# A two-block transformer kernel on one core: roots of three norms applied behind the products, roots computed as columns, four query tiles, key scores one step behind, four expert units ahead

## What is computed

```python
def rms_norm(x, g): return x * rsqrt(mean(x * x, -1) + EPS) * g

# first_block, two layers
h = rms_norm(x, norm_g[l]) * (1.0 + scale) + shift        # scale, shift from cond @ ada_w
# layer 0: z = h @ even_w_in; convolution of 31 taps and RWKV-7 recurrence; @ even_w_out
# layer 1: z = h @ odd_w_in; q, k, v, index heads; top-256 keys of each query; 16 heads; @ odd_w_out
x = x + gate * out
x = rms_norm(x, final_g)

# second_block
proj = rms_norm(h, g_mix) @ w_in                          # b_gate, c_gate, v_conv, u_pool
y_conv = b_gate * conv3(c_gate * v_conv)
y_pool = (window_mean(u_pool) - u_pool) @ pool_w * pool_scale
h = h + concat(y_conv, y_pool) @ w_o
xn = rms_norm(h, g_ffn)
s = (xn @ w_q) . sub_keys                                 # two top-16 lists, then top-16 of the 256 sums
gate = softmax(top_s)
h = h + sum_k gate * gelu(u[eidx] . xn) * v[eidx]
h = h + sigmoid(rms_norm(h, g_ple) @ w_ple_gate) * (p @ w_ple_proj)
out = rms_norm(h, g_final)
```

## Time and profile before

| what | us |
|---|---|
| runs, median of 3 (lowest, highest) | 3392.25 (3389.33, 3398.76) |
| the profiled execution's own time | 3389.65 |
| its span, from first to last instruction | 3387.7 |
| PE busy | 3124.9 (92%) |
| DVE busy | 2192.4 (65%) |
| ACT busy | 1232.9 (36%) |
| POOL busy | 888.4 (26%) |
| mean granted clock of PE | 0.963 of full speed |

### The profile page before, as it was taken

How to read it: one execution, slowest core, us unless ns; L and a number is a source line. 1 busy time by engine, 2 the same in 40 slices (tenths; PEclk the granted TensorE clock), 3 DMA queues, 4 the chain that set the end, 5 groups by cost and what they waited for, 6 DMA issues and landing times.

```text
span 3387.7 us, 39992 instructions
## 1 busy us (share of the span) xinstructions
PE 3124.9 (92%) x16218; PEld 2438.7 (72%) x16218; DVE 2192.4 (65%) x3471; ACT 1232.9 (36%) x1788; POOL 888.4 (26%) x548
## 2 busy tenths in 40 slices
PE   6799999998799799979899999999999999999996
PEld 3477777666587465757677788878888888888874
DVE  4689899754779855473679799936665444444445
ACT  3334444333323355323233366642222222223223
POOL 2344444310323110034335532232222111111100
PEclk9889999998889899989999999999999999999998
DMA  5311111324112110222223455675554333333320
GB/s 198 106 54 52 53 47 51 109 78 180 68 62 82 43 38 26 81 75 94 75 87 128 140 181 197 234 260 190 184 191 162 118 124 119 125 119 120 122 100 31
DMA packets 166615, 381.45 MB, mean 113 GB/s; under 512 B 10784, under 2 KB 77344, under 8 KB 166304
## 3 DMA queue, kind: packets, MB, share of 16 engines
q1 hardware_dynamic: 166432, 378.90, 33.4%
HBM read 319.62 MB, written 59.24 MB: 112 GB/s over the span
## 4 chain that ended last, share of the span: by engine, by line
PE 71%; DVE 20%; ACT 4%; POOL 2%; DMA 2%; issue 1%; SPq 0%; DVEq 0%; POOLq 0%; ACTq 0%
PE ps L667 20%; PE ps L669 19%; PE ps L668 19%; DVE rw L1672 4%; DVE oh L2213 2%; PE ps L1069 2%; PE ps L994 2%; DVE at L1954 1%; DVE ai L1952 1%; PE ps L974 1%; POOL wsp L2288 1%; PE ps L840 1%; DVE at L1942 1%; POOL pk L2389 1%; PE ps L984 1%
## 5 line engine op out<-in xcount | busy, mean ns | idle before, releaser
L667 PE MATMUL ps<-hT,wsp 128*128 128x512 f32 x2136 | 876.2, 410 | 86.2 <-POOL wsp L2288 37.0
L669 PE MATMUL ps<-hT,wsp 128*128 128x512 f32 x2136 | 846.5, 396 | 0.0
L668 PE MATMUL ps<-hT,wsp 128*128 128x512 f32 x2136 | 845.9, 396 | 0.0
L2288 POOL TENSOR_TENSOR wsp<-ring,wsp 128x1024 fp32r<-128x1024 f32 x205 | 510.8, 2494 | 1129.1 <-ACT wsp L1128 1128.9
L667 PEld LDWEIGHTS ps<-hT,wsp 128*128 128x128 f32 x2136 | 408.5, 191 | 206.4 <-issue 40.4
L669 PEld LDWEIGHTS ps<-hT,wsp 128*128 128x128 f32 x2136 | 408.8, 191 | 89.4
L668 PEld LDWEIGHTS ps<-hT,wsp 128*128 128x128 f32 x2136 | 410.2, 192 | 78.0 <-issue 1.4
L2396 POOL TENSOR_TENSOR ex<-ex 128x512 fp32r<-128x512 f32 x128 | 176.2, 1391 | 831.8 <-ACT ex L1487 831.8
L1128 ACT ACTIVATE wsp<-ring 128x1024 fp32r<-128x1024 f32 x312 | 322.5, 1050 | 89.6 <-PE ps L669 64.6
L2237 DVE TENSOR_TENSOR xT<-ps,xT 128x512 f32<-128x512 f32 x256 | 174.9, 688 | 265.0 <-PE ps L669 264.9
L667 PE MATMUL ps<-ex 128*128 128x512 f32 x808 | 315.1, 390 | 2.0 <-DVE ex L1537 2.0
(11 more groups left out here) (369 smaller groups left out, 4637.7 us busy)
## 6 DMA issues: line engine op xcount, KB each, us to landing
ring<-in_eu SPq DMA_DIRECT2D x128, 512.0 KB, 3.3
ring<-in_ev SPq DMA_DIRECT2D x128, 512.0 KB, 3.6
gd<-oh SPq DMA_DIRECT2D x8, 4096.0 KB, 15.1
ex<-gd SPq DMA_DIRECT2D x32, 1024.0 KB, 6.9
ring<-in_ein SPq DMA_DIRECT2D x57, 512.0 KB, 3.3
ring<-in_oin SPq DMA_DIRECT2D x40, 512.0 KB, 3.2
ring<-in_ada SPq DMA_DIRECT2D x37, 512.0 KB, 3.2
ex<-zd SPq DMA_DIRECT2D x17, 1024.0 KB, 9.2
```

What stands on the lines that cost most here:

```text
L667: pe.matmul(out, W[0], R[0], start=first, stop=False)
L668: pe.matmul(out, W[0], R[1], start=False, stop=False)
L669: return pe.matmul(out, W[1], R[0], start=False, stop=last)
L2288: pool.tensor_tensor(s[:, 1, :], raw_of(i), s[:, 0, :].bitcast(F32), ALU.subtract).then_inc(pool_done, G.step("lo", i))
```

## The change

1. **Roots behind the products.** For n2 with nx, nf and np the products run on the *raw* tiles, x times the gain (step `raw`: ACT makes the high part, DVE the low part, tile by tile as x becomes final). A product is linear, so the root of each token is multiplied on afterwards: on the bank for the mixer's units and the gate's (`pool_ev`, `bc`, `ple_ev`: 128x512 products on DVE with the root `R`, which ACT copies from PSUM), inside the exponential's scale for the softmax of nf (a token's order of scores does not depend on its root). `bg` and `cg` become `bc`. The expert units still use the normalised nf tiles in hT; they are made by `norm_nf` within the key steps, and the queries read a new buffer `hq`.
2. **Roots as columns.** `stat` now multiplies 128-token pieces of the sums with one column of ones (L754, four products of 128x1), so that scale, root and reciprocal work on 128x4 (`cr`); DVE spreads them on a diagonal (L1629), and `bcast` is the product with ones (L763) that puts the root on all partitions. ACT loads the root's table ahead by a root of a constant (`warm`). This holds for all norms; ident is loaded ahead of x for it.
3. **Attention.** `qTs` has four tiles; `q` is four heads ahead, three units stand ahead of the first `logits`; `ogs(0)` moves to head 12, and three output units `oo(0, 0..2)` fill heads 14 to 16.
4. **Key scores** (`keys`) stand one step behind the query units.
5. **Token blocks.** Four `pre` stand ahead of the first `cand`, and the one ahead of each `cand` is gone. ACT does the exponential in step `sums`, not in `gates`.
6. **End.** The projection's inputs are loaded ahead of the last chunk, `plep` is in two halves between the `ple` units; x is multiplied with the last gain on ACT (`xg`), and DVE multiplies with the spread root from PSUM.

The diff, cut to its core:

```diff
+    order += [("q", h, unit("oin", h)) for h in (1, 2, 3)]
     for h in range(17):
         if h < 16:
             order.append(("logits", h))
         if h:
             order.append(("pt", h - 1))
-        if h < 14:
-            order.append(("q", h + 2, unit("oin", h + 2)))
+        if h < 12:
+            order.append(("q", h + 4, unit("oin", h + 4)))
+        if h == 12:
+            order.append(("ogs", 0))
+        if h > 13:
+            order.append(("oo", 0, h - 14, unit("oout", 2 * (h - 14))))
...
+    order += [("oo", 0, m, unit("oout", 2 * m)) for m in range(3, 8)]
+    order.append(("freed", "n2"))
+    for m in range(8):
+        order.append(("oo", 1, m, unit("oout", 2 * m + 1)))
+        order += [("square", "n2", m), ("square", "nx", m)]
+        if m:
+            order.append(("raw", "n2", m - 1))
+    order.append(("raw", "n2", 7))
+    pin = [unit("win", 12 + g) for g in range(4)]
+    order += [("pool_in", 0, pin[0]), ("stat", "n2"), ("stat", "nx"), ("pool_in", 1, pin[1])]
+    order += [("mx_begin",), ("bcast", "nx"), ("bcast", "n2"), ("pool_ev", 0, pin[0])]
+    order += [("pool_in", 2, pin[2]), ("pool_ev", 1, pin[1]), ("pool_in", 3, pin[3]), ("pool_ev", 2, pin[2])]
+    for m in range(8):
+        order.append(("bc", m, unit("win", m)))
+        if m == 0:
+            order.append(("pool_ev", 3, pin[3]))
+        order.append(("res", m))
     order += [("vc", m, unit("win", 8 + m)) for m in range(4)]
     order.append(("pool_out",))
     order.append(("yms",))
     for m in range(8):
         order.append(("wo", m, unit("wo", m)))
         order.append(("square", "nf", m))
-    order.append(("stat", "nf"))
-    order.append(("pk_begin",))
-    order.append(("norm", "nf"))
+        if m:
+            order.append(("raw", "nf", m - 1))
+    order += [("raw", "nf", 7), ("freed", "nf"), ("pk_begin",)]
...
-    for hp in range(16):
-        order.append(("wq", hp, unit("wq", hp)))
-        order.append(("keys", hp))
+    for hp in range(17):
+        if hp < 16:
+            order.append(("wq", hp, unit("wq", hp)))
+        if hp == 0:
+            order.append(("stat", "nf"))
+        if hp == 1:
+            order.append(("bcast", "nf"))
+        if hp:
+            order.append(("keys", hp - 1))
+        if 4 <= hp < 14:
+            order.append(("norm_nf", hp - 4))
+    for _ in range(4):
+        pre()
     for blk in range(4):
-        pre()
         order.append(("cand", blk))
...
+        if c == NC - 1:
+            order += [("p_in",), ("freed", "np")]
         order.append(("v", c, [unit("ev", c * JC + j) for j in range(JC)]))
-    order.append(("stat", "np"))
-    order.append(("plep",))
-    order.append(("norm", "np"))
+    pln = [unit("pleg", m) for m in range(8)]
+    order += [("ple", 0, pln[0]), ("stat", "np"), ("ple", 1, pln[1]), ("bcast", "np"), ("plep", 0)]
     for m in range(8):
-        order.append(("ple", m, unit("pleg", m)))
-        order.append(("square", "ng", m))
-    order.append(("stat", "ng"))
+        if m >= 2:
+            order.append(("ple", m, pln[m]))
+        order.append(("ple_ev", m, pln[m]))
+        if m == 1:
+            order.append(("plep", 1))
+        if m:
+            order += [x for k in ((0, 1) if m == 1 else (m,)) for x in (("square", "ng", k), ("xg", k))]
+    order += [("stat", "ng"), ("bcast", "ng")]
...
-        qTs = [b(512) for _ in range(2)]
+        qTs = [b(512), b(512), *att[12:14]]
...
+                for b in range(4):
+                    r = pe.matmul(out[:, b:b + 1], acc_of[tag][:, b * 128:(b + 1) * 128], ones[:, 0:1], start=True, stop=True)
+                r.then_inc(tensor_done, T.step("sum", tag))
+            def bcast(tag):
+                reader = (A, "R", tag) if tag in kept else (V, "out", 7) if tag == "ng" else (V, "x", tag, 7)
+                out, free = (inv_b if tag == "n0" else all_b).open(("bc", tag), *reader)
+                w.wait_ge(*free)
+                w.wait_ge(vector_done, V("diag", tag))
+                pe.matmul(out, ones[:, :], acc_of[tag], start=True, stop=True).then_inc(tensor_done, T.step("bc", tag))
...
+            def stat(tag):
+                i = tags.index(tag)
+                w.wait_ge(scalar_done, A.was("warm", i - 4))
+                act.activation(cr[:, 12 + i % 4:13 + i % 4], ones[:, 0:1], ACT.Sqrt).then_inc(scalar_done, A.step("warm", i))
                 w.wait_ge(vector_done, V("mean", tag))
-                act.activation(ap, ap, ACT.Sqrt).then_inc(scalar_done, A.step("rt", tag))
+                act.activation(root_of[tag], root_of[tag], ACT.Sqrt).then_inc(scalar_done, A.step("rt", tag))
+            def bcast(tag):
+                if tag in kept:
+                    w.wait_ge(tensor_done, T("bc", tag))
+                    act.activation(acc_of[tag], all_b.at["bc", tag], ACT.Copy).then_inc(scalar_done, A.step("R", tag))
...
                 gt = ijg[:, 256:384]
                 w.wait_ge(vector_done, V("gt", blk))
-                act.activation(gt, gt, ACT.Exp).then_inc(scalar_done, A.step("gexp", blk))
+                w.wait_ge(vector_done, V("rs", "nf"))
+                act.activation(gt, gt, ACT.Exp, scale=root_of["nf"][:, blk:blk + 1]).then_inc(scalar_done, A.step("gexp", blk))
...
                 w.wait_ge(scalar_done, A("rt", tag))
-                dve.reciprocal(ap, ap).then_inc(vector_done, V.step("rs", tag))
+                dve.reciprocal(r, r).then_inc(vector_done, V.step("rs", tag))
+                own()
+                dve.tensor_tensor(acc_of[tag].rearrange("p (b n) -> p b n", b=4),
+                                  ident[:, :].rearrange("p (o n) -> p o n", o=1).broadcast_to([128, 4, 128]),
+                                  r.rearrange("p (b o) -> p b o", o=1).broadcast_to([128, 4, 128]), ALU.mult).then_inc(
+                    vector_done, V.step("diag", tag))
...
+                dve.scalar_tensor_tensor(out=raw_h[tag][:, 1, k, :], in0=xT[:, k, :], scalar=gain[tag][:, k:k + 1],
+                                         in1=raw_h[tag][:, 0, k, :].bitcast(F32), op0=ALU.mult, op1=ALU.subtract).then_inc(
+                    vector_done, V.step("raw", tag, k))
...
+                w.wait_ge(scalar_done, A("R", "nx"))
+                dve.tensor_tensor(z[:, PADL:PADL + S], all_b.at[n], m2, ALU.mult).then_inc(vector_done, V.step("pz", g))
...
+            def bc(m, n):
+                lo_to(n + 1)
+                w.wait_ge(tensor_done, T("use", n))
+                if m == 4:
+                    dve.tensor_tensor(mxt[0], m2, m2, ALU.mult).then_inc(vector_done, V.step())
+                    own()
+                dve.tensor_tensor(*((ym[:, m, :], all_b.at[n], m2) if m < 4 else (mxt[6 + m], all_b.at[n], mxt[0])),
+                                  ALU.mult).then_inc(vector_done, V.step("bc", m))
...
+            def ple_ev(m, n):
+                own()
+                w.wait_ge(tensor_done, T("use", n))
+                w.wait_ge(scalar_done, A("R", "np"))
+                dve.tensor_tensor(exb[m % 4], all_b.at[n], msum, ALU.mult).then_inc(vector_done, V.step("pr", m))
...
+                    dve.tensor_tensor(xT[:, k, :], xT[:, k, :], all_b.at["bc", "ng"], ALU.mult).then_inc(
```

## The result

The changed kernel takes 3308.78 us (median of 4 runs, 3301.39 to 3314.57), the kernel before 3393.95 (4 runs beside it): ratio 0.9748, 95% interval 0.9718 to 0.9777. Forecast were 3311 us, range 3292 to 3338. The profiled execution of the change took 3301.39 us (span 3299.5), against 3389.65: 88.3 us less, of which the medians show 85.

The account below looks back on a forecast made before the run. TensorE, busy 92% of the span, was taken as the bound, with time won only where it idles or runs at its lower clock. Terms summed to 81 us, giving 3311 us, range 3292 to 3338.

Parts of the forecast that it names:

- first norm: At the start: it waits for the modulation's loads, not the root; gain 0, between -1 and +1 us.
- second norm: Order stays, only the root's chain gets shorter, 8.2 to 4.9 us: gain 3.3 us.
- attention: Query units cover the 18.81 us wait for tile 1, but first transposes come 5.6 us later: gain 7, ends 1 and 13.
- mixer: Output products to pooling: units start at once, one unit about 3 us late remains: gain 27 us, ends 18 and 30.
- norm ahead of queries: Stretch of 22.0 us ahead of the queries, less one unit and the sums and spreading: gain 14.5 us.
- key scores: One step behind the query units, 16 waits of 0.69 us go, VectorE just fits: gain 10 us, ends 1 and 11.
- token blocks: Block 0 costs 1.2 us, blocks 1 to 3 cost 4.2 each: loss 3, ends loss 12 and gain 6.
- last two norms, tail: End of the kernel: 82.5 us become 61.4, gain 21, ends 14 and 23; tail 10.4 to 9.4, gain 1.
- Rival B: VectorE and GpSimd hold each other up in key steps, token blocks and mixer: 3337 us, chance 0.20.
- Rival C: All cover holds: token blocks cost 1.2 us each, attention gains 12: 3297 us, chance 0.20.
- Rival E: Long busy stretches no longer granted clock 1.00, each per cent costing 31 us: 3436 us at 4 per cent, chance 0.01.
- Rival D: PE runs out of its eight banks before the root arrives, 8 us in each of three stages: 3335 us, chance 0.07.

Follow-up runs that it names:

- p_keys: Kernel before, with only each query block moved one ahead of its key scores: 3376.19 against 3390.88 us, ratio 0.9962.
- u_keys: Changed kernel with each query block's key scores again right behind the block: 3325.19 us, ratio to the kernel before 0.9807.
- l_44: Changed kernel with GpSimd's lookup cut in two, four products, the next weight split, then the other four: 3309.53 us.
- d_look: Changed kernel with all 16 lookup products of a block on VectorE, none on GpSimd: 3313.87 us, ratio to the kernel before 0.9769.
- last version: Changed kernel with the first norm behind two of four groups of modulation rows and the hot tiles' table loaded a stage earlier: 3305.06 us, ratio 0.9743.
- old blocks: Changed kernel with one unit ahead of each token block, not four ahead of the first, and the exponential ahead of the lookup: 3310.96 us.
- d_both: Changed kernel with the whole lookup and the weight splits of the hot stretch and later expert units on VectorE: 3601.51 us, ratio 1.061.
- n_early: Changed kernel with identity load behind x, first norm's spreading product behind all modulation rows, its column sums behind two groups: 3307.7 us.

## Why the prediction was right, and where it was not

The total was right, and in part by luck: the terms miss by amounts of both signs, and two that no term forecast, -4.1 ahead of the second norm and +3.9 in the hot tiles and experts, happen to cancel. In us, predicted and from the profiled executions:

| term | predicted | measured |
|---|---|---|
| first norm | 0 | -2.3, and -1.8 up to the second norm |
| second norm | 3.3 | 3.7 |
| attention | 7 | 6.0 |
| mixer | 27 | 29.1 |
| norm ahead of queries, key scores | 14.5 + 10 | 15.7 + 12.2 |
| token blocks | -3 | +0.6 |
| hot tiles, experts | none | 3.9 |
| last two norms, tail | 21 + 1 | 21.0 + 0.2 |
| sum | 81 | 88.3 |

- **Second norm, last norms**: right to half a microsecond, including the 1.3 us at the seventh projection tile (1.37). The tail gave 0.2 in place of 1: PE waits 4.81 us for ScalarE in front of the last sums.
- **Attention**: the size was right and undoing it costs 7 to 11.5, but not by the path forecast. Of the two waits near 8 us only the first came; the second is 0.69, and the heads without a query unit wait 3.3 each, as counted. The first transposes come 2.5 us later, not 5.6. With the wait ahead of the loop, PE's waits above 0.3 us fall from 31.6 to 19.9 us, by 11.8, and the stage by 6.0 only. At least part of the rest went to the low clock, which the term left out: the first head's transposes now come in pieces with waits of 0.3 to 0.7 us between them, and the granted clock is 0.50 for the ten microseconds behind 1148, in which PE gets through 20 products; before it was 1.00 at the same place, with 39 products. Windows of the change and of before (busy of PE, PEld, DVE, ACT, POOL, granted clock, DMA share, GB/s):
```profile
1148.00:1158.00 10.00, 7.10 (x20) 5.23 (x20) 8.25 (x21) 6.20 (x14) 2.35 (x1) 0.50 0.16 52
```
```profile
1143.00:1153.00 10.00, 7.36 (x39) 5.78 (x37) 8.26 (x21) 6.20 (x14) 2.35 (x1) 1.00 0.17 52
```
- **Mixer**: right. The one wait of 3 us for a weight split was not there; a wait of 1.33 for VectorE was. With 617.7 to 622.3 us for A-B in equal code, 27 and 29.1 are not to be told apart.
- **Key scores**: the term counted the waits (0.69) and took 0.1 off for the thick steps; a step saved 0.81, since the product behind a wait is slower as well (1.16 us against 1.05). At one pace of the units it is 0.94 to 0.95 (p_keys, u_keys); the change's own steps give 0.14 of it back to a slower pace, told below.
- **Token blocks, the step that failed**: "Before: 5.7 + 1.5 + 3 x 1.2 = 10.8. Now 1.2 + 3 x 4.2". The 4.2 was too much: the waits for GpSimd are 1.2, then 2.6, 2.4 and 2.3 us, with the lookup at 6.5 to 6.9 us and not 7 to 9. With them the same sum gives 8.6, a gain of 2.2 where the trace has 0.6, and 206.9 less 204.6 to 206.4, or 0.5 to 2.3, by all traces of the code. What the sum can't do is say what the stage gives when such a wait is taken away: in l_44 6.4 us of waits for GpSimd went and waits for VectorE and ScalarE of the same size came, and in d_look it was so again. It would be too simple to say that the stage ends when VectorE ends. VectorE stands still itself for 20.9 of the 206.3 us in the change, in waits for the lookup, for ScalarE and for a load; its timeline has:
```profile
1744.68 2.29 DVE L2228 TENSOR_REDUCE pk<-pk 128x128 f32<-128x2048 f32 x1 [6.33 <-POOL pk L2459]
...
1880.26 2.28 DVE L2250 CAST px<-px 128x1024 bf16<-128x1024 f32 x1 [5.65 <-ACT px L1496]
1888.50 2.17 DVE L2277 TENSOR_TENSOR oh<-oh,px 128x2048 bf16<-128x2048 bf16 x1 [3.05 <-DMA oh<-in_iom]
```
The last of them lies behind PE's 2.05 us at the first hot products: the last version, with the table loaded earlier, has neither wait. Five orders of this stage (before, change, old blocks, l_44, d_look) took 204.6 to 210.9 us; the two traces over 207 (old blocks and p_keys) are those with a wait of 8.62 us in block 0. (In d_both, 212.1 us, it is the wait of 8.8 us at the first hot products.) That the four units ahead spare PE this wait fits, but no run moves them alone.
- **Rival B** had the mechanism right and the place wrong. VectorE is held by GpSimd by the length of a GpSimd operation, also where it costs PE nothing. Timeline of the change, GpSimd's split and VectorE's operations beside and behind it:
```profile
1897.07 2.57 POOL L2362 TENSOR_TENSOR wsp<-ring,wsp 128x1024 fp32r<-128x1024 f32 x1 [3.01 <-ACT wsp L1163]
```
```profile
1897.33 3.39 DVE L2277 TENSOR_TENSOR oh<-oh,px 128x2048 bf16<-128x2048 bf16 x1
...
1905.31 1.22 DVE L2277 TENSOR_TENSOR oh<-oh,px 128x2048 bf16<-128x2048 bf16 x1
```
The first began 0.26 us behind the split, and ended 1.08 behind its end: nearly all of its 1.22 us ran only then. By the Trainium skill, page SBUF — State Buffer, section "Who interferes with whom", the one is shut out until the other ends; here the trace agrees (3.39 against 1.22). In the key steps it cost PE nothing: no step has a wait.
- **Rival C**, all cover holds, came halfway at most: the blocks' waits are 2.3 to 2.6 us where it had 1.2, and the attention gave 6.0 us where it had 12.
- **Rival E** did not come: granted clock 1.00 from 2300 to 3100 us. **Rival D** did not either: no wait for the root's copy.

The 3.9 us of the hot tiles and the experts, and 1.8 ahead of the second norm, are scatter, not the change: equal code differs by as much. In D-E it goes with the clock: 250.6 us at a granted 0.97 in before, 247.4 at 0.99 in the change, 244.8 at 1.00 with before's code in p_keys.

## What to carry to other kernels

A norm's root can stand behind products that don't need it, and moving the chain behind one unit of work saves more than the wait, since PE also stays at the high clock: opening the chain cost 8.6 us for 3.9 us of waits ahead of the queries, 6.0 us for 5.0 of waits ahead of the gate. In a stage where PE, VectorE and GpSimd hand work to each other all the time, PE's waits tell what the stage costs, but not what removing one of them gives: ask first which wait stands behind it. And before giving an engine another's work to relieve it, read what then stands behind that work in its queue.

## What the runs showed of the hardware

- **The clock's rise can differ from run to run.** Behind the same waits of 1.7 us, a row of equal products reached the full clock at 872.6 us in before, 3.1 behind its start, and at 878.4 in the change, 6.4 behind its start. In the other twelve traces it came 3.0 to 3.4 behind, also with the change's code. PE in before and in the change:
```profile
869.42 0.80 PE L667 MATMUL ps<-hT,wsp 128*128 128x512 f32 x1 [1.69 <-DVE hT L1829]
...
872.55 0.39 PE L668 MATMUL ps<-hT,wsp 128*128 128x512 f32 x1
```
```profile
872.01 0.80 PE L704 MATMUL ps<-hT,wsp 128*128 128x512 f32 x1 [1.70 <-DVE hT L1895]
...
878.43 0.40 PE L704 MATMUL ps<-hT,wsp 128*128 128x512 f32 x1
```
That alone makes 1.5 us over the 24 products from there. Between traces of equal code the stages differ by similar amounts (1.8 us in C-D, 3.1 in D-E, 2.3 in E-F), while the fastest and the slowest run of the change lie 13 us apart. An effect of 2 us is seen in a stretch, if at all, never in the total.
- **Two paces at one clock.** With the granted clock at 1.00, two products of a unit start 0.227 us apart in many stretches, but 0.233 in the queries of the change, and in pieces of other stretches of both kernels. A key step is 6.50 us in the change and 6.36 where the same order stands alone on the kernel before: 2 us in 15 steps. This is not scatter, as u_keys and n_early have 0.233 in the queries too. These three kernels read the new buffer `hq` there, the kernel before reads hT; whether that sets the pace is not tested.
